# Other places for the modulation chunks, the head sums and the tile splits in the read-out of a two-direction recurrence

## The chip, the cores and the metric

The kernel runs on one core of a Trainium2 chip. The metric is the device time in microseconds (us) of the whole program. The program is cut into stages by barriers at which all engines but SyncE meet, and the change touches three neighbouring stages (the two directions of a recurrence and their read-out).

## The reference, cut to what matters

The reference computes two transformer blocks over 512 tokens of 1024 features. The change lies in the first block. There, modulation vectors (shift, scale and gate of each sublayer) come from the conditioning vector `c`, and a mixer joins an attention half and a gated recurrence that runs in both time directions:

```python
mod_x = (silu(c) @ w_mod[l] + b_mod[l])[:, None, :]
sh1, sc1, gt1, sh2, sc2, gt2 = jnp.split(mod_x, 6, axis=-1)
...
hg_x, hg_c = hgrn2_mixer(px[3:], pc[3:], lb_all[l], hg_norm[l], need_ctx)   # both directions
x = x + gt1 * (concatenate([na_x, hg_x], -1) @ w_out[l])
x = x + gt2 * peer_ffn(modulate(rms_norm(x, norm2[l]), sh2, sc2), ...)

def _gated_out(o, g, norm_g):      # o: sum of both directions, per head
    o = o * rsqrt(mean(o * o, -1) + EPS) * norm_g
    o = o * silu(g)
```

`sh1` and `sc1` are needed at the start of the block. The other four vectors of `mod_x`, which are two thirds of the columns of `w_mod`, are needed only after the recurrence: `gt1` at the output projection, the rest behind it. `peer_ffn` later gathers rows of two tables, `peer_u` and `peer_v`, by index.

## The kernel before

**Weights.** All weights come as one stream of chunks of 512 KB (`in_wstream`), numbered in the order of use. The ring `RING` has four slots (`NSLOT`). SyncE issues the load of chunk c as soon as chunk c-4 has been used, which TensorE reports by the semaphore `chunk_used`. Chunks 48 to 79 are the 32 modulation chunks of the second call (`mod2` and `mod3`), 80 to 87 are the output projection (`out`), and 88 to 103 come after it (`wq`).

**Copies on the same queue.** Behind the load of a chunk SyncE issues copies of the two tables, interleaved row by row, into a DRAM tensor `peer_uv` (L396): each copy takes 1 MB from DRAM to DRAM. From chunk 48 to 79 there is one copy behind each chunk, and two behind each chunk whose number is a multiple of four; from chunk 80 on there is one. These copies are in no hurry, since `peer_uv` is read much later, but they lie in one queue with the loads.

**Modulation** (`modulation`, L611; its matmuls are L617). `modulate(n)` takes the next n of the 32 modulation chunks: 8 matmuls for each chunk with 32 stationary columns (the conditioning) and 128 moving columns from the ring slot, summed up in PSUM bank 6 or 7. It uses no other engine. The author places these calls by hand into gaps of TensorE. Once all 32 are done, ScalarE copies the rows out (`evacuate_rows`, L1146), TensorE turns them (`turn_rows`, L625), and VectorE adds the bias (`add_bias`).

**Two directions** (loop over `d`, one stage each). VectorE runs 24 scans (L1596) and computes 1 - Z (L1598), which sets `ready`. TensorE then makes 16 groups of 8 products (L743), x = 0 to 15; from x = 2 on each waits for VectorE, which scales the operands (L1619, L1620) and takes the last group's result under a mask (`take`, L1608). After each odd x there is one `modulate(1)`. Then TensorE turns six blocks (L756), which ScalarE copies out and VectorE needs to go on, multiplies for the state update (L762), and VectorE carries the state (L1634, L1638) up to the barrier. Before: `modulate(6)` stands ahead of the wait for `ready` in both directions.

**Read-out.** For each of four heads TensorE makes 16 products (L771, L773) into one bank, ScalarE copies and squares it (L1263, L1264). TensorE then runs `modulate(4)` and the four sums over the squares by a matrix of ones (L779). ScalarE takes the four roots (L1115, L1117), VectorE normalises and gates each head (L1647, L1649) and splits the first three chunks of `out` into a high and a low part (`first_chunks`, L1469 and L1471). Barrier 6 follows. Behind it VectorE splits tiles 4 to 7 of `MIX` (the four heads; tiles 0 to 3 were split at the start of the stage; L1485, L1487). TensorE runs eight matmuls that only keep its clock up (`keep_clock`, L634, 512 columns of an identity each), and the tiles of `out` begin (L204 to L206, three passes for each pair of parts).

The order of work on each engine is the order of the program text. Nothing is scheduled by a planner.

Of the kernel before, what the change touches and what calls it, by code (L numbers as in the profile page):

```python
# [20 lines left out]
ALU = mybir.AluOpType  # L21
# [5 lines left out]
KT = D // P  # L27
# [8 lines left out]
HG_HEADS, HG_UNIT = 4, 128  # L36
# [74 lines left out]
def build(nc, t):  # L111
    ctx = ExitStack()
    place = {}
    with ctx:
        def sb(name, shape, dt=F32):
            x = ctx.enter_context(nc.sbuf_tensor(name, shape, dt))
            n = int(np.prod(shape[1:])) * (1 if dt == U8 else 4)
            place[name] = (nc.sbuf_base - n, list(shape))
            return x
# [7 lines left out]
        def sem(name):  # L127
            return ctx.enter_context(nc.semaphore(name))
# [7 lines left out]
        IDN, ONES = sb("IDN", [P, P]), sb("ONES", [P, P])  # L136
# [13 lines left out]
        def bank(b, a=0, n=512):  # L150
            return PS[:, b * 512 + a:b * 512 + a + n]

        def ar(a, n):
            return AR[:, a:a + n]

        def par(name):
            a, n = PCOL[name]
            return PAR[:, a:a + n]
# [12 lines left out]
        def barrier(eng, n):  # L171

            eng.drain().then_inc(phase, 1)  # L173
            eng.wait_ge(phase, 4 * n)
# [41 lines left out]
        G = ar(21504, 2048).rearrange("p (a b) -> p a b", a=4)  # L216
        VW = ar(12288, 4096).rearrange("p (a b) -> p a b", a=4)
        VC = ar(16384, 1024).rearrange("p (a b) -> p a b", a=4)
        MIX = ar(23552, 4096).rearrange("p (a b) -> p a b", a=8)
# [35 lines left out]
        def unit(d, j, h):  # L255

            n = [4, 5, 0, 1, 2, 3][j] if d == 0 else [5, 4, 3, 2, 1, 0][j]
            return (TT * h + n if n < TT else 4 * TT + 2 * h + n - TT), n
# [5 lines left out]
        HLF, HCF, XCF = (x[:].rearrange("p k s -> p (k s)") for x in (HL, HC, XC))  # L264
# [98 lines left out]
        def after(eng, s, key, n, per):  # L363

            eng.wait_ge(s[key], s["use"] * per + n)
# [8 lines left out]
        ho = {k: sem(f"ho_{k}") for k in ("o", "sq", "sum", "root")}  # L374
# [144 lines left out]
        def _(pe):  # L519
# [91 lines left out]
            def modulation(c, which, b):  # L611

                for i in which:
                    weights(pe, c + i)
                for k in range(KT):
                    for i in which:
                        mm = pe.matmul(row_of(bank(b), i), CS[:, 2 * k:2 * k + 32], part(RING, c + i, P * k, P),  # L617
                                       start=(k == 0), stop=(k == KT - 1), skip_group_check=True)
                mm.then_inc(chunk_used, len(which))

            def turn_rows(n, b):

                pe.wait_ge(mod_rows, n + 1)
                for j in range(4):
                    mm = pe.transpose(bank(b, P * j, P), MROWS[n][:, P * j:P * j + P], IDN[:])  # L625
                mm.then_inc(mod_turned, 1)
# [4 lines left out]
            def keep_clock(b, n):  # L631

                for _ in range(n):
                    pe.matmul(bank(b), IDN_R[:], eyes, start=True, stop=True)  # L634
# [91 lines left out]
            def modulate(n):  # L726
                for _ in range(n):
                    i = next(made)
                    modulation(FIRST["mod2"], [i], 6 + i // 16)

            for d in range(2):
                s = hg[d]
                modulate(6)
                after(pe, s, "ready", 1, 1)
                for x in range(16):
                    half = x % 2
                    if x >= 2:
                        after(pe, s, "p", x - 1, 16)
                        after(pe, s, "qk", x - 1, 14)
                    for u in range(8):  # L740
                        a = (8 * half + u) * P
                        lhs, rhs = (Z[d], HQ) if x < 2 else (QK, QK)
                        mm = pe.matmul(PS[:, a:a + P], lhs[:, a:a + P], rhs[:, a:a + P], start=True, stop=True)  # L743
                    mm.then_inc(s["a"], 1)
                    if x % 2 == 1:
                        modulate(1)
                keep_clock(5, 6)
                for n, b in enumerate(HG_BLOCKS):
                    if n == 2:
                        after(pe, s, "p", 16, 16)  # L750
                    if 2 <= n < 5:
                        keep_clock(3, 2)
                    after(pe, s, "kd", n + 1, 6)
                    for j in range(4):
                        a = 512 * b + P * j
                        mm = pe.transpose(PS[:, a:a + P], EW[:, a:a + P], IDN[:])  # L756
                    mm.then_inc(s["kt"], 1)
                after(pe, s, "kz", 6, 6)
                for j in range(5):
                    for h in range(HG_HEADS):  # L760
                        u, n = unit(d, j, h)
                        mm = pe.matmul(bank(j, P * h, P), Z[d][:, u * P:u * P + P], IV[:, n, P * h:P * h + P],  # L762
                                       start=True, stop=True)
                    mm.then_inc(s["u"], 1)
                barrier(pe, 4 + d)

            for h in range(HG_HEADS):
                for n in range(TT):
                    u = (TT * h + n) * P
                    for d in range(2):  # L770
                        pe.matmul(bank(h, P * n, P), IV[:, n, P * h:P * h + P], AT[d][:, u:u + P], start=(d == 0),  # L771
                                  stop=False)
                        mm = pe.matmul(bank(h, P * n, P), SS[d][:, h, n, :], QE[d][:, u:u + P], start=False,  # L773
                                       stop=(d == 1))
                mm.then_inc(ho["o"], 1)
            modulate(4)
            for h in range(HG_HEADS):
                pe.wait_ge(ho["sq"], h + 1)
                pe.matmul(bank((4, 5, 1, 0)[h]), ONES[:], HLF[:, 2048 + 512 * h:2560 + 512 * h], start=True,  # L779
                          stop=True).then_inc(ho["sum"], 1)  # L780
            turn_rows(1, 3)
            turn_rows(2, 4)
            barrier(pe, 6)
            keep_clock(1, 8)

            tiles(FIRST["out"], KT, MIXS, "mix1", main, n2, follow=rms(n2))
            passing(pe, 7)
# [27 lines left out]
            for tt in range(TT):  # L815
                if tt >= 2:
                    pe.wait_ge(po_evac, 2 * (tt - 1))
                for j in range(SLOTS):
                    n = SLOTS * tt + j
                    pe.wait_ge(diag_ready, n + 1)  # L820
                    for x in range(2):
                        mm = pe.matmul(bank(2 * (tt % 2) + x), DIAG[:, n % NDIAG, :],  # L822
                                       ROWS_UV[n % NROW][:, D + 512 * x:D + 512 * x + 512], start=(j == 0),
                                       stop=(j == SLOTS - 1))
# [636 lines left out]
        def _(dve):  # L1461
            steps = Steps(dve, dve_step)
# [12 lines left out]
            def first_chunks(name):  # L1475
                for c in range(ahead):
                    split_chunk(FIRST[name] + c)
# [5 lines left out]
            def split_tile(x, hi, lo, to, n=1):  # L1483

                steps.done(dve.tensor_copy(hi, x))  # L1485
                steps.wait()
                dve.tensor_tensor(lo, x, hi.bitcast(F32), ALU.subtract).then_inc(to, n)  # L1487
# [5 lines left out]
            def split_mix(*which):  # L1493
                for k in which or range(KT):
                    split_tile(MIX[:, k, :], MIXS[0][:, k, :], MIXS[1][:, k, :], x_split)
# [148 lines left out]
            for h in range(HG_HEADS):  # L1644
                o, r = HLF[:, 512 * h:512 * h + 512], EW[:, 512 * h:512 * h + 512]
                dve.wait_ge(ho["root"], h + 1)
                steps.done(dve.tensor_tensor(o, o, r, ALU.mult))  # L1647
                steps.wait()
                dve.scalar_tensor_tensor(MIX[:, 4 + h, :], o, par("hg_norm")[:, h:h + 1], G[:, h, :], ALU.mult, ALU.mult)  # L1649
            first_chunks("out")  # L1650
            barrier(dve, 6)


            split_mix(*range(4, KT))
            for n in (1, 2):
                steps.done(add_bias(n, n + 2))
            steps.wait()
# [156 lines left out]
            for i in range(RET_HEADS * TT):  # L1814
                pair, j = divmod(i // 2, TT)
                h, n = 2 * pair + i % 2, S - P * j
# [108 lines left out]
            for c in range(16):  # L1925
                split_chunk(FIRST["dq"] + c + ahead)
                dve.wait_ge(chunk_used, FIRST["dq"] + c + 1)
                h, by = c % 8, (1.0 if c >= 8 else 0.125)
# [21 lines left out]
            for i in range(n_df + 5):  # L1950
# [16 lines left out]
                if i >= 5:  # L1967
                    k = i - 5
                    o = DO[:, k // TT, P * (k % TT):P * (k % TT) + P]
# [5 lines left out]
                if i % TT == 0 and 1 <= i // TT <= DIFF_HEADS - DLATE:  # L1975
                    h = DLATE + i // TT - 1
# [4 lines left out]
            for h in range(DBY_POOL, DIFF_HEADS):  # L1981
                dve.wait_ge(df["root"], h + 1)
                for ib in range(TT):
                    o = DO[:, h, P * ib:P * ib + P]
# [142 lines left out]
```

## Time and profile before

| | us |
|---|---|
| time before, median of 3 runs | 3511.51 (3508.32 to 3514.45) |
| the profiled execution | 3522.56 |
| its span in the trace | 3520.8 |
| first direction, from barrier 3 to 4 | 390.6 to 480.3 |
| second direction, from barrier 4 to 5 | 480.3 to 563.4 |
| read-out, from barrier 5 to 6 | 563.4 to 599.2 |
| busy in the span: TensorE, VectorE | 3024.0, 2070.3 |

The times in the rows are from the start of the span. The three stages together take 209 us, 6% of the kernel. TensorE has two clocks, and in these stages the granted clock is between 0.64 and 1.00 over stretches of 10 us; a matmul of 512 columns that keeps the clock starts every 0.25 us at the fast one and every 0.45 us at the slow one.

### The profile page before, as it was taken

What the parts mean: (1) busy time and instruction counts of PE and PEld (TensorE: products, weight loads), DVE (VectorE), ACT (ScalarE), POOL (GpSimd) and SP (SyncE); (2) the same over time, 40 slices, a digit from 0 to 9 for tenths busy, and PEclk for the clock granted to TensorE, in tenths of its full rate; (3) what the DMA queues carried; (4) which work ended last, traced back from release to release, by engine and by line L of the source; (5) the groups of instructions that cost most, each with busy time, mean ns of one, the idle gap of its engine ahead of it and who ended that gap; (6) DMA issues with size and microseconds to landing.
All of it is one profiled execution on the core that took longest, in us unless ns stands there. A gap on an engine that the chain in (4) does not pass through costs nothing.

```text
span 3520.8 us, 35290 instructions
## 1 busy us (share of the span) xinstructions
PE 3024.0 (86%) x12520; PEld 2047.1 (58%) x12520; DVE 2070.3 (59%) x3646; ACT 834.3 (24%) x2176; POOL 703.5 (20%) x682
## 2 busy tenths in 40 slices
PE   7999888987777777777777789979999999899998
PEld 5886677762222222222222257667888777778876
DVE  3224785567776764684444455356875465668743
ACT  2112432222222222222222231142120102422201
POOL 0002452014444443343433311000000000100000
PEclk9999999999999999999999999989999999999999
DMA  6999896769999999999999942202333231023332
GB/s 220 317 290 296 242 293 218 234 252 421 421 421 421 408 418 422 413 414 419 419 417 421 415 197 90 78 1 80 99 96 90 78 114 54 12 80 95 95 90 72
DMA packets 154613, 847.89 MB, mean 241 GB/s; under 512 B 15392, under 2 KB 15648, under 8 KB 87648
## 3 DMA queue, kind: packets, MB, share of 16 engines
q0 software_dynamic: 79360, 563.38, 39.3%
q1 hardware_dynamic: 75104, 282.57, 25.9%
q8 instruction: 87, 1.43, 0.2%
q14 instruction: 62, 0.51, 0.0%
HBM read 841.70 MB, written 136.31 MB: 278 GB/s over the span
## 4 chain that ended last, share of the span: by engine, by line
PE 57%; DMA 27%; DVE 8%; issue 4%; ACT 3%; SPq 0%; ACTq 0%; POOL 0%; DVEq 0%; POOLq 0%
DMA RHI_f<-peer_uv,XC 19%; PE PS L204 13%; PE PS L206 13%; PE PS L205 13%; PE PS L822 7%; DMA AR<-peer_uv,XC 5%; DMA RING<-in_wstream 3%; PE PS L597 1%; PE PS L617 1%; DVE AR L1678 1%; DVE RING_r L1471 1%; DVE AR L1608 1%; ACT HC L1315 1%; PE PS L634 1%; DVE AR L1620 1%
## 5 line engine op out<-in xcount | busy, mean ns | idle before, releaser
L822 PE MATMUL PS<-AR,HC 128*128 128x512 f32 x1536 | 726.5, 618 | 256.9 <-ACT HC L1315 256.9
L204 PE MATMUL PS<-AR_r,RHI 128*128 128x512 f32 x1888 | 751.5, 398 | 26.6 <-DVE RING_r L1471 8.9
L206 PE MATMUL PS<-AR_r,RING_r 128*128 128x512 f32 x1888 | 737.7, 391 | 0.0
L822 PEld LDWEIGHTS PS<-AR,HC 128*128 128x128 f32 x1536 | 284.2, 194 | 698.5 <-ACT HC L1315 403.2
L1678 DVE SCALAR_TENSOR_TENSOR AR<-AR 128x1024 f32<-128x1024 f32 x384 | 470.1, 1225 | 366.8 <-DMA AR<-peer_uv,XC 366.2
L205 PE MATMUL PS<-AR_r,RHI 128*128 128x512 f32 x1504 | 586.2, 390 | 0.0
L488 POOL DMA_INDIRECT AR<-peer_uv,XC x384 | 400.3, 1042 | 729.1 <-PE PS L822 547.9
L1469 DVE CAST RHI<-RING 128x1024 fp32r<-128x1024 f32 x256 | 178.4, 697 | 485.4 <-DMA RING<-in_wstream 482.8
L204 PEld LDWEIGHTS PS<-AR_r,RHI 128*128 128x128 f32 x1888 | 356.2, 189 | 111.0 <-issue 21.2
L206 PEld LDWEIGHTS PS<-AR_r,RING_r 128*128 128x128 f32 x1888 | 355.8, 188 | 74.4
L1471 DVE TENSOR_TENSOR RING_r<-RING,RHI 128x1024 fp32r<-128x1024 f32 x256 | 315.8, 1234 | 8.8
L205 PEld LDWEIGHTS PS<-AR_r,RHI 128*128 128x128 f32 x1504 | 282.9, 188 | 62.9 <-issue 6.0
L822 PE MATMUL PS<-RHI_f,HC 128*128 128x512 f32 x512 | 236.7, 605 | 80.8 <-ACT HC L1315 80.8
L1306 ACT ACTIVATE XC<-XC 128x2 f32<-128x2 f32 x256 | 52.1, 203 | 926.6 <-DVE AR L1678 926.6
L1678 DVE SCALAR_TENSOR_TENSOR AR<-RHI_f,AR 128x1024 f32<-128x1024 f32 x128 | 156.6, 1225 | 119.6 <-DMA RHI_f<-peer_uv,XC 119.4
L822 PEld LDWEIGHTS PS<-RHI_f,HC 128*128 128x128 f32 x512 | 92.3, 190 | 225.2 <-ACT HC L1315 133.0
L1315 ACT ACTIVATE HC<-IDN,HC 128x128 f32<-128x128 f32 x512 | 173.7, 386 | 0.0
L488 POOL DMA_INDIRECT RHI_f<-peer_uv,XC x128 | 133.7, 1045 | 186.1 <-PE PS L822 182.3
L205 PE MATMUL PS<-HL_r,RHI 128*128 128x512 f32 x384 | 151.4, 394 | 0.0
L1309 ACT ACTIVATE HC<-XC 128x1 f32<-128x1 f32 x512 | 122.9, 287 | 8.4
L1391 ACT ACTIVATE HL<-PS,PAR 128x512 f32<-128x512 f32 x88 | 67.8, 777 | 228.0 <-PE PS L206 184.4
L506 POOL DMA_DIRECT2D AR<-in_strips x1 | 0.7, 672 | 572.7 <-DVEq L173 572.7
(337 smaller groups left out, 3457.9 us busy)
## 6 DMA issues: line engine op xcount, KB each, us to landing
RING<-in_wstream SPq DMA_DIRECT2D x304, 512.0 KB, 3.6
peer_uv<-in_peer_u SPq DMA_DIRECT2D x56, 1024.0 KB, 14.7
peer_uv<-in_peer_v SPq DMA_DIRECT2D x56, 1024.0 KB, 16.6
peer_uv<-in_peer_v POOLq DMA_DIRECT2D x8, 1024.0 KB, 11.9
peer_uv<-in_peer_u POOLq DMA_DIRECT2D x8, 1024.0 KB, 11.9
AR<-peer_uv,XC POOLq DMA_INDIRECT x384, 13.5
XL<-in_xl SPq DMA_DIRECT2D x1, 2048.0 KB, 8.1
RHI_f<-peer_uv,XC POOLq DMA_INDIRECT x128, 13.5
```

The lines of the kernel that those rows point to most:

```text
L204: pe.matmul(out, sh, mh, start=start, stop=False)
L205: pe.matmul(out, sh, ml, start=False, stop=False)
L206: return pe.matmul(out, sl, mh, start=False, stop=stop)
L488: pool.indirect_dma_start(ROWS_UV[n % NROW], None, PEER_UV, bass.IndirectOffsetOnAxis(ap=IDX[:, n:n + 1], axis=0)).then_inc(row_landed[n % ...
L822: mm = pe.matmul(bank(2 * (tt % 2) + x), DIAG[:, n % NDIAG, :], ROWS_UV[n % NROW][:, D + 512 * x:D + 512 * x + 512], start=(j == 0), stop= ...
L1306: act.activation(GA[:, n:n + 2], RAW[:, n:n + 2], ACT.Gelu).then_inc(gelu, 1)
L1309: act.activation(WEIGHT[:, n + x:n + x + 1], GA[:, n + x:n + x + 1], ACT.Copy, scale=GATE[:, n + x:n + x + 1]).then_inc(weight_ready, 1)
L1315: act.activation(DIAG[:, (n + x) % NDIAG, :], IDN[:], ACT.Copy, scale=WEIGHT[:, n + x:n + x + 1]).then_inc(diag_ready, 1)
L1391: act.activation(HL[:, x, :], bank(x % 4), ACT.Identity, scale=PAR[:, bass.ds(g * BLK + (cw + 2 * 2 * FT + x), 1)], bias=PAR[:, bass.ds(g ...
L1469: dve.tensor_copy(hi, x).then_inc(w_high, 1)
L1471: dve.tensor_tensor(lo, x, hi.bitcast(F32), ALU.subtract).then_inc(w_split, 1)
L1678: dve.scalar_tensor_tensor(JUNK[n % 2], ROWS_UV[n % NROW][:, 0:D], 1.0, HT[:, n // SLOTS, :], ALU.mult, ALU.mult, accum_out=RAW[:, n:n + 1 ...
```

## The change

Five things change, four on TensorE and one on VectorE:

- In direction 0 no modulation chunk comes ahead of `ready`; 36 matmuls of `keep_clock` stand there instead. In direction 1 four chunks stand there, where there were six.
- After the 16 groups, direction 0 takes four more chunks and direction 1 two, both ahead of the transposes; `keep_clock` behind them goes from 6 to 4.
- In the read-out the sum of head h-1 follows the products of head h, and the last sum follows at the end. The remaining modulation chunks, six where there were four, come behind the sums.
- The barrier comes ahead of `turn_rows`, and `keep_clock` behind goes from 8 to 4.
- VectorE splits a head's tile right behind its gating, where it split all four behind the barrier.

The 32 chunks are 14, 14 and 4 before, and 12, 14 and 6 after (direction 0, direction 1, read-out). Nothing changes in SyncE's, ScalarE's or GpSimd's program.

```diff
--- before.py
+++ after.py
@@ -730,7 +730,10 @@
 
             for d in range(2):
                 s = hg[d]
-                modulate(6)
+                if d == 0:
+                    keep_clock(5, 36)
+                else:
+                    modulate(4)
                 after(pe, s, "ready", 1, 1)
                 for x in range(16):
                     half = x % 2
@@ -744,7 +747,8 @@
                     mm.then_inc(s["a"], 1)
                     if x % 2 == 1:
                         modulate(1)
-                keep_clock(5, 6)
+                modulate(4 if d == 0 else 2)
+                keep_clock(5, 4)
                 for n, b in enumerate(HG_BLOCKS):
                     if n == 2:
                         after(pe, s, "p", 16, 16)
@@ -764,6 +768,11 @@
                     mm.then_inc(s["u"], 1)
                 barrier(pe, 4 + d)
 
+            def head_sum(h):
+                pe.wait_ge(ho["sq"], h + 1)
+                pe.matmul(bank((4, 5, 1, 0)[h]), ONES[:], HLF[:, 2048 + 512 * h:2560 + 512 * h], start=True,
+                          stop=True).then_inc(ho["sum"], 1)
+
             for h in range(HG_HEADS):
                 for n in range(TT):
                     u = (TT * h + n) * P
@@ -773,15 +782,14 @@
                         mm = pe.matmul(bank(h, P * n, P), SS[d][:, h, n, :], QE[d][:, u:u + P], start=False,
                                        stop=(d == 1))
                 mm.then_inc(ho["o"], 1)
-            modulate(4)
-            for h in range(HG_HEADS):
-                pe.wait_ge(ho["sq"], h + 1)
-                pe.matmul(bank((4, 5, 1, 0)[h]), ONES[:], HLF[:, 2048 + 512 * h:2560 + 512 * h], start=True,
-                          stop=True).then_inc(ho["sum"], 1)
+                if h >= 1:
+                    head_sum(h - 1)
+            head_sum(HG_HEADS - 1)
+            modulate(6)
+            barrier(pe, 6)
             turn_rows(1, 3)
             turn_rows(2, 4)
-            barrier(pe, 6)
-            keep_clock(1, 8)
+            keep_clock(1, 4)
 
             tiles(FIRST["out"], KT, MIXS, "mix1", main, n2, follow=rms(n2))
             passing(pe, 7)
@@ -1646,12 +1654,13 @@
                 dve.wait_ge(ho["root"], h + 1)
                 steps.done(dve.tensor_tensor(o, o, r, ALU.mult))
                 steps.wait()
-                dve.scalar_tensor_tensor(MIX[:, 4 + h, :], o, par("hg_norm")[:, h:h + 1], G[:, h, :], ALU.mult, ALU.mult)
+                steps.done(dve.scalar_tensor_tensor(MIX[:, 4 + h, :], o, par("hg_norm")[:, h:h + 1], G[:, h, :], ALU.mult,
+                                                    ALU.mult))
+                steps.wait()
+                split_mix(4 + h)
             first_chunks("out")
             barrier(dve, 6)
 
-
-            split_mix(*range(4, KT))
             for n in (1, 2):
                 steps.done(add_bias(n, n + 2))
             steps.wait()
```

On TensorE, from the last work of the attention stage into direction 0 (L709 is that stage's; L743, after L746, are the products; L617 the modulation). Before:

```order
L709 MATMUL PS<-HL,AR 64x128 x8
L617 MATMUL PS<-RING,CS 32x128 x48
L743 MATMUL PS<-AR 128x128 x16
L617 MATMUL PS<-RING,CS 32x128 x8
L743 MATMUL PS<-AR 128x128 x16
```

and after, with the end of the 16 groups of the same direction:

```order
L709 MATMUL PS<-HL,AR 64x128 x8
L634 MATMUL PS<-IDN_R 128x512 x36
L746 MATMUL PS<-AR 128x128 x16
L617 MATMUL PS<-RING,CS 32x128 x8
...
L746 MATMUL PS<-AR 128x128 x16
L617 MATMUL PS<-RING,CS 32x128 x40
L634 MATMUL PS<-IDN_R 128x512 x4
L760 MATMUL PS<-IDN,AR 128x128 x8
```

Six chunks have left the head of the direction, and four of them stand between the last products and the first transposes (x40 is five chunks, where one stood before).

On TensorE, from the last products of the read-out to the first tile of `out`. Before:

```order
L773 MATMUL PS<-AR,HC 128x128
L617 MATMUL PS<-RING,CS 32x128 x32
L779 MATMUL PS<-HL,ONES 128x512 x4
L625 MATMUL PS<-IDN,AR 128x128 x4
L625 MATMUL PS<-IDN,STAT 128x128 x4
L634 MATMUL PS<-IDN_R 128x512 x8
L204 MATMUL PS<-AR_r_57,RHI 128x512
```

and after:

```order
L782 MATMUL PS<-AR,HC 128x128
L773 MATMUL PS<-HL,ONES 128x512 x2
L617 MATMUL PS<-RING,CS 32x128 x48
L625 MATMUL PS<-IDN,AR 128x128 x4
L625 MATMUL PS<-IDN,STAT 128x128 x4
L634 MATMUL PS<-IDN_R 128x512 x4
L204 MATMUL PS<-AR_r_57,RHI 128x512
```

The sums (L779, after L773) now stand ahead of the chunks, two of the four further up among the products, and six chunks stand where four did.

## Rows read from the trace of the kernel before

**Rows 1.** Busy time by stretch, all engines, then granted clock, DMA share and GB/s.

```profile
410.00:475.00 65.00, 58.08 (x439) 52.09 (x438) 53.90 (x51) 21.04 (x26) 37.81 (x30) 0.95 1.02 331
...
568.00:580.00 12.00, 12.00 (x109) 11.88 (x108) 0.00 (x0) 3.69 (x7) 0.00 (x0) 1.00 0.00 1
```

**Rows 2.** Timeline of TensorE, direction 0: start, length, work, [idle before <- releaser].

```profile
390.59 7.66 PE L617 MATMUL PS<-RING,CS 128*32 128x128 f32 x80 [0.44 <-DVEq L173]
407.38 3.62 PE L617 MATMUL PS<-RING,CS 128*32 128x128 f32 x16 [9.13 <-DMA RING<-in_wstream]
410.93 4.87 PE L743 MATMUL PS<-AR 128*128 128x128 f32 x32
464.12 2.01 PE L617 MATMUL PS<-RING,CS 128*32 128x128 f32 x16
466.06 1.65 PE L634 MATMUL PS<-IDN_R 128*128 128x512 f32 x6
467.55 1.03 PE L756 MATMUL PS<-IDN,AR 128*128 128x128 f32 x8
```

**Rows 3.** Timeline of VectorE: the instruction that sets `ready`, in each direction.

```profile
401.06 1.74 DVE L1598 TENSOR_SCALAR AR<-AR 128x3072 f32<-128x3072 f32 x1
...
488.02 1.73 DVE L1598 TENSOR_SCALAR AR<-AR 128x3072 f32<-128x3072 f32 x1
```

**Rows 4.** Timeline of TensorE, direction 1.

```profile
480.32 8.91 PE L617 MATMUL PS<-RING,CS 128*32 128x128 f32 x80 [2.15 <-DVEq L173]
492.62 3.62 PE L617 MATMUL PS<-RING,CS 128*32 128x128 f32 x16 [3.39 <-DMA RING<-in_wstream]
496.17 4.91 PE L743 MATMUL PS<-AR 128*128 128x128 f32 x32
549.16 1.66 PE L634 MATMUL PS<-IDN_R 128*128 128x512 f32 x6
```

**Rows 5.** DMA view, issues at 423.9, 430.5, 466.2, 483.0, 510.0: KB, us to landing.

```profile
RING<-in_wstream SPq DMA_DIRECT2D x1, 512.0 KB, 19.4
RING<-in_wstream SPq DMA_DIRECT2D x1, 512.0 KB, 16.3
RING<-in_wstream SPq DMA_DIRECT2D x1, 512.0 KB, 10.6
RING<-in_wstream SPq DMA_DIRECT2D x1, 512.0 KB, 3.8
RING<-in_wstream SPq DMA_DIRECT2D x1, 512.0 KB, 22.7
```

**Rows 6.** Timeline of TensorE, read-out and first tile of `out`.

```profile
563.40 0.80 PE L771 MATMUL PS<-AR 128*128 128x128 f32 x2 [2.13 <-DVEq L173]
...
579.46 5.95 PE L617 MATMUL PS<-RING,CS 128*32 128x128 f32 x64
585.34 3.70 PE L779 MATMUL PS<-HL,ONES 128*128 128x512 f32 x8
...
599.22 3.78 PE L634 MATMUL PS<-IDN_R 128*128 128x512 f32 x8 [5.97 <-DVEq L173]
602.79 0.63 PE L204 MATMUL PS<-AR_r,RHI 128*128 128x512 f32 x1
```

**Rows 7.** The four chunk loads issued in the read-out: lines of L411, 581 to 586.

```profile
L411 SPq DMA_DIRECT2D RING<-in_wstream x4: 333/334/334, 581.4 to 585.4; - x4
...
DMA to landing us min/median/max: 3.6/10.0/16.2
```

**Rows 8.** Timelines of ScalarE and VectorE in the read-out.

```profile
580.06 0.59 ACT L1264 ACTIVATE HL<-PS 128x512 f32<-128x512 f32 x1
586.50 0.69 ACT L1115 ACTIVATE AR<-PS,PAR 128x512 f32<-128x512 f32 x1 [5.86 <-PE PS L779]
...
592.78 0.75 DVE L1649 SCALAR_TENSOR_TENSOR AR<-HL,PAR,AR 128x512 f32<-128x512 f32 x1
...
599.25 0.43 DVE L1485 CAST AR_r<-AR 128x512 fp32r<-128x512 f32 x1
```

## The prediction, made before the changed kernel had run

> **What bounds the kernel now.** The change lies in three stages, which one barrier after the other keeps in line, so first the timeline of TensorE was read there, then who releases its waits, and then, since a load releases the two longest, the loads themselves. Between the barriers VectorE paces the 16 groups of products. From the first group of direction 0 to its last modulation chunk pass 53.2 us (410.93 to 464.12) [rows 2], and 53.0 us in direction 1 up to the end of its last one (496.17 to 549.16) [rows 4]. The heads of both directions are set by a load. In direction 0 `ready` comes at 402.8 [rows 3], but the sixth chunk lands only at 407.4, and the first products start at 410.93 [rows 2]. In direction 1 `ready` comes at 489.8 [rows 3], the sixth chunk at 492.6, the products at 496.17 [rows 4]. That is 8.1 and 6.4 us which the order of the chunks costs TensorE.
>
> Behind these waits stands a full queue: the DMA engines are at a share of 1.02 from 410 to 475 [rows 1]. On an empty queue a load lands 3.6 to 3.8 us after its issue [rows 5, 7], here after 10.6 to 22.7 [rows 5]. Copies issued between the loads take the time. I number chunks from the program: 59 is the load issued at 423.9, 65 at 466.2, 66 at 483.0, 73 at 510.0, and 80 to 83 are the four of the read-out. Issue plus time to landing gives 443.3 for 59, 476.8 for 65, 486.8 for 66 and 532.7 for 73 [rows 5]. In the read-out the first lands at 585.0 and the fourth at 601.6, so a step of one load and one copy takes 16.6 / 3 = 5.5 us [rows 7]. From 59 to 73 there are 14 steps, four of them with a second copy; they took 33.5 us (59 to 65) and 45.9 us (66 to 73), and the step between, in which the queue ran dry, would have taken some 5.3: 84.7 us, 6.05 a step. The groups use a chunk every 6.5 us (51 to 53 us for eight). The queue and the loop are nearly balanced: what the queue loses by standing idle it cannot make up.
>
> **Direction 0.** Without a chunk ahead, the first group starts with `ready`, at 402.9: **8.0 us earlier**. The 36 clock matmuls hide: at 0.25 us each (six take 466.06 to 467.55 [rows 2]) they end at 399.5. At the slow clock they take 0.45 us (eight take 599.22 to 602.79 [rows 6]), 16.1 in all, and would end at 406.7 and cost 3.8 of the 8.0. I take the fast one, since the chunks that stood there ran at 0.19 us a pair of records, twice as fast as chunk 53's 0.45 [rows 2]. They leave TensorE idle for 3.4 us. Idle gaps of 2.13 and 2.15 us were followed by slow matmuls [rows 4, 6], so I count no gain from the clock in the first groups, which ran at the slow one before as well (4.87 us [rows 2]).
>
> The four added chunks stand between the last products and the transposes, and for these ScalarE waits and then VectorE; no work hides them. Four in a row take 5.9 us (579.46 to 585.34 [rows 6]); two clock matmuls fewer give back 0.5. Transposes, and with them the barrier, come 8.0 - 5.4 = **2.6 us earlier**, and direction 1 starts at 477.7 for 480.3. The last of the four, chunk 59, is issued when 55 has been used, at 458.1, and lands on an empty queue at 461.7; TensorE wants it at 462.4.
>
> **Direction 1.** `ready` comes at 489.75 - 2.6 = 487.1. The queue has been given 60 to 63 by then: four steps of 6.05 behind 461.7 put chunk 63 at 485.9. It is the last of the four ahead of `ready`. TensorE has waited for it for 3 us and takes 3.6 us at the slow clock, like chunk 67 (3.62 [rows 4]). The products start at 489.5, not at 487.1: **6.7 us earlier** than before, not 9.1. 53.0 us later, at 542.5, the loop is done. Two more chunks follow. Chunk 72 is used by 544.0. Chunk 73 is 14 steps behind 59: 461.7 + 84.7 = 546.4. It takes 3.6 us slow, then four clock matmuls 1.8, and the transposes start at 551.8. Before it was 549.16 + 1.49 = 550.65 [rows 2, 4]. So direction 1 gives all of the gain back, and the read-out starts **1.1 us later**, at P = 564.5 (before 563.40 [rows 6]). The reason is in the head of direction 0: the first load went out at 392.5 there, and now goes out when chunk 48 has been used in the loop, at 409.7. The queue stands idle for 17 us more.
>
> **Read-out.** Head sums take 3.70 / 4 = 0.93 us each [rows 6]. Two now lie among the products and put the last square from P + 17.3 (580.65 [rows 8]) to P + 19.1; the last sum follows, and the chunks begin at P + 20.0, before at P + 16.1. The roots begin at P + 19.1 for P + 23.1 (586.50 [rows 8]), 4.0 us earlier. VectorE is done with the heads 7.0 us behind (593.5 [rows 8]), plus four splits of 0.43 + 0.69 [rows 8]: P + 30.6 for P + 30.1. So the earlier sums are paid away by the splits, which before came behind the barrier, where TensorE had 8 us of tiles for which parts were ready.
>
> Then VectorE must split chunks 80, 81 and 82, and barrier 6 waits for that. This is **the largest term**. 82 can be issued only when 78 has been used. Before, 78 and all others had landed, four chunks were used in a row, and 80, 81, 82 were issued from 581.4 and landed by 596.1 [rows 7], 1.2 us ahead of VectorE. Now chunks 78 and 79 are not there: they are issued when 74 and 75 have been used, the first two of the six, and the queue has been dry before, as now [rows 1]. From the start of the chunks to the first issue pass 2.0 us (579.46 to 581.4), then 3.6 to 78, then four steps of 5.5 to 82: P + 20.0 + 2.0 + 3.6 + 22.2 = P + 47.8. One split is 1.9 us (three between 593.5 and 599.2), so the barrier falls at P + 49.7. Before it was P + 35.8 (599.22 [rows 6]): **13.9 us later**. TensorE's and ScalarE's ends, about P + 34, lie under it. `turn_rows` behind the barrier is 1.0 to 1.8 us and four clock matmuls are 1.8, against 3.57 before [rows 6]: 0.3 us less.
>
> **Sum.** 1.1 + 13.9 - 0.3 = 14.7 us later at the first tile of `out`. Behind it the tiles use the first chunk some 16 us later, by when the queue is empty again as before; each stage starts at a barrier, and so the shift goes through to the end. The profiled execution took 3522.56 us, with a span of 3520.8; it lies 11 us over the median, spread over all stages, so I add the difference to the median: 3511.5 + 14.7 = 3526.2 us.
>
> **A rule against the rows.** The read-out's step is 5.5 us by its row [rows 7]. The Trainium skill, "DMA: Bandwidth & Descriptors", section "Anatomy of one DMA — SWDGE (gpsimd) path", fits 2.0 us plus bytes at 436 GB/s to a transfer; a load and a copy of 1.57 MB in all would add 3.6 us a step. The rows don't bear that out as a mean; a copy reads and writes DRAM, and the rate there is what the landings show.
>
> **Rivals.** (A) The queue binds in the read-out alone: loads 63 and 73 are there in time. Then direction 1 starts its products with `ready` at 487.1, the transposes begin at 487.1 + 53.0 + 2.9 + 1.0 = 544.0, and P = 556.8, 6.6 us earlier. The sum is -6.6 + 13.9 - 0.3 = +7.0: 3518.5. For it speaks that 73 misses by only 2.4 us; against it, 63 by 3.
> (B) Not slower: the queue drains faster once copies are thinner spread. The step from the load issued at 423.9 to that at 430.5 was 3.5 us (446.8 - 443.3 [rows 5]). If all were so, no chunk is late in the directions (-6.6), 82 lands at P + 20.0 + 2.0 + 3.6 + 14 = P + 39.6, the barrier is at P + 41.5, and the sum -6.6 + 5.7 - 0.3 = -1.2: 3510.3. This is also what the page's fit would give. Against it stands every mean over more than one step.
> (C) Faster: chunks are never late, barrier 6 waits for VectorE alone, at P + 30.6 + 5.7 = P + 36.3. The sum is -6.6 + 0.5 - 0.3 = -6.4, and 1 or 2 us more if the clock holds: 3504. It needs 82 within 14 us of the first issue, 78 ahead of it.
> (D) More: steps of 5.9 in the read-out (+1.6), 59 issued on a queue that isn't empty, and slow clock in the loops (+6): 3534.
>
> **How the numbers follow.** The forecast has 0.66, A 0.10, B 0.07, C 0.04, D 0.13. The forecast's own range is 3521 to 3531. The range of 8 in 10 takes in A and most of D: 3516 to 3535. A difference of 0.2% (7 us) is about what a measurement of this kernel tells from none. C is the chance of faster, 0.04; B and half of A lie within, 0.12; the rest is slower, 0.84.
>
> **What the profile after would show.** In direction 0 the products start near 402.9, and the first load goes out near 409.7. In direction 1 the fourth chunk (63) waits for its load. Behind the 16 groups of direction 1 the third modulation chunk waits for a load. In the read-out TensorE waits for its last two chunks, and VectorE's splits of 80 to 82 wait for their loads, about 5 us apart; barrier 6 comes about 50 us behind the first product, for 36. The forecast is wrong if VectorE goes from the heads into `first_chunks` without idle time, or if a step of load and copy takes less than 4.5 us.

## The result, and the profile after

| | before | changed |
|---|---|---|
| median | 3511.51 us (3508.32 to 3514.45) | 3527.67 us (3525.45 to 3529.31) |
| ratio | | 1.0044 (95% interval 1.0030 to 1.0059) |
| profiled execution, its span | 3522.56, 3520.8 us | 3529.05, 3527.3 us |

The changed kernel is 16.2 us slower by the medians, where 14.7 us were forecast (3526). Measured again beside the experiments it stood at 1.0043 (1.0026 to 1.0059).

The two traces don't start alike: barrier 3 opens direction 0 at 390.6 us before and at 388.0 after, so times below are taken from there. Each column is one execution. How far single executions differ up to the read-out is shown in the part on why the prediction was right, and it changes how the first rows of this table are to be read.

| us from the start of direction 0 | before | changed | difference | forecast |
|---|---|---|---|---|
| first products of direction 0 | 20.3 | 12.3 | -8.1 | -8.0 |
| VectorE's first masked copy (`take`) | 23.5 | 16.4 | -7.1 | |
| direction 1 starts | 89.7 | 86.1 | -3.7 | -2.6 |
| first products of direction 1 | 105.6 | 101.2 | -4.4 | -6.7 |
| transposes of direction 1 | 160.1 | 158.5 | -1.5 | +1.1 |
| read-out starts (P) | 172.8 | 171.3 | -1.5 | +1.1 |
| barrier 6 | 208.6 | 222.1 | +13.5 | +15.0 |
| first tile of `out` | 212.2 | 225.6 | +13.4 | +14.7 |

TensorE in direction 0 and at the head of direction 1 of the changed kernel (start, length, work, [idle before <- releaser]); these rows answer to [rows 2, 4]:

```profile
387.95 8.46 PE L634 MATMUL PS<-IDN_R 128*128 128x512 f32 x36 [0.44 <-DVEq L173]
400.22 6.46 PE L746 MATMUL PS<-AR 128*128 128x128 f32 x32 [3.81 <-DVE AR L1606]
...
452.71 7.57 PE L617 MATMUL PS<-RING,CS 128*32 128x128 f32 x80
...
461.24 1.03 PE L760 MATMUL PS<-IDN,AR 128*128 128x128 f32 x8
...
474.01 4.90 PE L617 MATMUL PS<-RING,CS 128*32 128x128 f32 x32 [2.14 <-DVEq L173]
479.90 1.93 PE L617 MATMUL PS<-RING,CS 128*32 128x128 f32 x16 [0.99 <-DMA RING<-in_wstream]
485.56 3.62 PE L617 MATMUL PS<-RING,CS 128*32 128x128 f32 x16 [3.72 <-DMA RING<-in_wstream]
```

The wait of 9.13 us for a load at the head of direction 0 is gone; the products wait for L1606, which sets `ready`. In direction 1 two of the four chunks wait for loads, the last for 3.72 us, and it runs at the slow clock as the late ones did before.

The end of direction 1 and the read-out on TensorE, against [rows 4, 6]:

```profile
543.58 1.93 PE L617 MATMUL PS<-RING,CS 128*32 128x128 f32 x16 [0.44 <-DMA RING<-in_wstream]
...
559.23 0.70 PE L780 MATMUL PS<-AR 128*128 128x128 f32 x2 [2.13 <-DVEq L173]
...
578.30 1.12 PE L773 MATMUL PS<-HL,ONES 128*128 128x512 f32 x2 [0.31 <-ACT HL L1272]
579.36 7.57 PE L617 MATMUL PS<-RING,CS 128*32 128x128 f32 x80
591.36 3.62 PE L617 MATMUL PS<-RING,CS 128*32 128x128 f32 x16 [4.43 <-DMA RING<-in_wstream]
610.10 1.11 PE L625 MATMUL PS<-IDN,AR 128*128 128x128 f32 x4 [15.12 <-DVEq L173]
```

VectorE in the same stretch, against [rows 8] (the last head's split, then the splits of chunks 80 to 82):

```profile
589.22 0.69 DVE L1495 TENSOR_TENSOR AR_r<-AR,AR_r 128x512 fp32r<-128x512 f32 x1
596.79 0.69 DVE L1477 CAST RHI<-RING 128x1024 fp32r<-128x1024 f32 x1 [6.88 <-DMA RING<-in_wstream]
...
602.03 0.69 DVE L1477 CAST RHI<-RING 128x1024 fp32r<-128x1024 f32 x1 [3.29 <-DMA RING<-in_wstream]
...
608.04 0.69 DVE L1477 CAST RHI<-RING 128x1024 fp32r<-128x1024 f32 x1 [4.06 <-DMA RING<-in_wstream]
```

And the loads of chunks 78 to 82, issued from 581.3 to 587.0 (the lines of L411 in that window), against [rows 7]:

```profile
L411 SPq DMA_DIRECT2D RING<-in_wstream x5: 333/693/1089, 581.3 to 587.0; - x5
...
DMA to landing us min/median/max: 3.6/12.8/21.1
```

The first lands at 584.9 and the last at 608.1: four steps of 5.8 us, each one load and one copy. VectorE waits 14.2 us in all for the three last of them, and TensorE stands idle for 15.12 us up to barrier 6. Before, VectorE went from the heads into these splits without a pause.

### The profile page after: what moved, and what is told of

Same layout as the page of the kernel before. It is cut to its first block and busy times, and to the rows that moved or that the text cites. A ratio compares the mean times of both kernels' runs of the same rounds, so it can differ in the third digit from the quotient of the medians.

```text
span 3527.3 us, 35347 instructions
## 1 busy us (share of the span) xinstructions
PE 3025.1 (86%) x12548; PEld 2048.1 (58%) x12548; DVE 2071.3 (59%) x3646; ACT 834.5 (24%) x2176; POOL 700.5 (20%) x682
## 5 line engine op out<-in xcount | busy, mean ns | idle before, releaser
L204 PE MATMUL PS<-AR_r,RHI 128*128 128x512 f32 x1888 | 751.2, 398 | 22.7 <-DVE RING_r L1479 7.9
## 6 DMA issues: line engine op xcount, KB each, us to landing
peer_uv<-in_peer_u POOLq DMA_DIRECT2D x8, 1024.0 KB, 16.2
```

Source lines behind the costliest of these rows:

```text
L204: pe.matmul(out, sh, mh, start=start, stop=False)
```

## The experiments

My theory: the queue of the DMA engines sets the ends of these stages, and only where a load stands behind copies and somebody waits for it. The main rival: the new order costs time on the engines themselves. Each run was measured beside the kernel before, and its ratio is to that; it can differ by some 0.0002 from the quotient of two medians, and the interval behind it is of 95%. A microsecond is 0.028 points (per cent).

### The five copies in the way, moved

The changed kernel, with the copies behind chunks 78 to 82 issued behind chunk 91, after which SyncE has nothing to issue for 17 us. Four of the five stand ahead of chunk 82; the fifth comes right behind it.

```diff
         _more = 2 if _c % 4 == 0 and _c < FIRST["out"] else 1
+    if FIRST["out"] - 2 <= _c < FIRST["out"] + 3:
+        _more = 0
+    elif _c == FIRST["wq"] + 3:
+        _more = 6
```

> The changed kernel with one thing else: the five table copies behind chunks 78 to 82 are issued behind chunk 91 instead (six there), where the queue would stand idle. Theory (the read-out waits for loads that stand behind copies): chunks 78 to 82 then land about 1.3 us apart, VectorE doesn't wait for 80 to 82, barrier 6 comes 36.4 us behind the first product of the read-out instead of 50.8, and the kernel takes 3513 us, ratio to the kernel before 1.000. Rival (the new order costs time on the engines themselves, by the splits ahead of the barrier and the chunks behind the sums): no change against the changed kernel, 3527 us, ratio 1.0045.

Measured: 3514.58 us, ratio 1.0004 (0.9995 to 1.0013). TensorE's read-out, the first split of a chunk on VectorE, and the time to landing of the six loads issued from 579.6 to 587.1:

```profile
557.49 0.78 PE L784 MATMUL PS<-AR 128*128 128x128 f32 x2 [2.13 <-DVEq L177]
...
577.62 9.50 PE L621 MATMUL PS<-RING,CS 128*32 128x128 f32 x96
593.87 0.48 PE L629 MATMUL PS<-IDN,AR 128*128 128x128 f32 x1 [6.75 <-DVEq L177]
```

```profile
588.09 0.69 DVE L1481 CAST RHI<-RING 128x1024 fp32r<-128x1024 f32 x1
```

```profile
L415 SPq DMA_DIRECT2D RING<-in_wstream x6: 327/328/334, 579.6 to 587.1; - x6
...
DMA to landing us min/median/max: 3.5/4.4/5.4
```

The engines' instructions and their order are the same; loads land 3.5 to 5.4 us after their issue, all six chunks run through in 9.50 us, VectorE waits for none, and barrier 6 comes 36.4 us behind the first product for 50.9, to the tenth as expected. Taken together the engines' own order costs nothing that can be measured; what makes the changed kernel slower are these copies. Its parts are not each without effect: by the prediction the early sums gain 4.0 us and the splits ahead of the barrier cost 4.5, and a run further down, with four chunks at the end and without those splits, has barrier 6 at 30.5 us. The run doesn't tell either whether the loads were late because they stood behind the copies in SyncE's order or because both shared the DMA engines at that time; no run moved the copies to another queue.

The same move in the kernel before:

> The kernel before with the five copies behind chunks 78 to 82 issued behind chunk 91, and nothing else. It tells whether moving these copies is a gain by itself. Theory (a copy costs only where somebody waits for the load behind it): in the kernel before chunk 82 landed 1.2 us ahead of VectorE, so nothing is gained, barrier 6 stays 35.8 us behind the first product, ratio 1.000. Rival (less traffic there helps in general, and gave the 14 us in the changed kernel): faster by 5 us or more, ratio 0.998 or less.

Measured: 3513.66 us, ratio 0.9997 (0.9986 to 1.0007). Barrier 6 stays where it was, 35.9 us behind the first product (560.06 to 595.94). So it isn't that less traffic there helps in general. The copies cost 14 us only in an order in which somebody waits behind them.

### One part of the change alone: the early head sums

The kernel before, with the sums among the products and `modulate(4)` behind them:

```diff
                 mm.then_inc(ho["o"], 1)
-            modulate(4)
-            for h in range(HG_HEADS):
-                pe.wait_ge(ho["sq"], h + 1)
...
+                if h >= 1:
+                    head_sum(h - 1)
+            head_sum(HG_HEADS - 1)
+            modulate(4)
```

> The kernel before with one part of the change alone: each head's sum follows the next head's products, and the four chunks come behind the sums. Theory (loads set the barrier): the roots start 4.0 us earlier, but the loads of chunks 80 to 82 are issued 3.9 us later, chunk 82 lands 36.7 us behind the first product and barrier 6 comes at 38.6 for 35.8: 2.8 us slower, ratio 1.0008. Rival (the chain of sums, roots and VectorE sets it): 4.0 us faster, ratio 0.9989.

Measured: 3518.77 us, ratio 1.0016 (1.0006 to 1.0025). TensorE, then VectorE's splits of 81 and 82:

```profile
555.35 0.49 PE L776 MATMUL PS<-AR 128*128 128x128 f32 x2 [2.13 <-DVEq L173]
...
593.14 3.78 PE L634 MATMUL PS<-IDN_R 128*128 128x512 f32 x8 [11.98 <-DVEq L173]
```

```profile
586.05 0.69 DVE L1473 CAST RHI<-RING 128x1024 fp32r<-128x1024 f32 x1 [4.52 <-DMA RING<-in_wstream]
...
591.09 0.69 DVE L1473 CAST RHI<-RING 128x1024 fp32r<-128x1024 f32 x1 [3.09 <-DMA RING<-in_wstream]
```

Barrier 6 is 37.8 us behind the first product for 35.8. These 2.0 us lie at the lower end of what the ratio says (2 to 9 us). A step that makes the roots start 4 us earlier makes the kernel slower, since it puts off the chunks that release the loads. Then with both edits, sums and moved copies:

> The kernel before with the early head sums (as in the run that had this part alone, 1.0016) and the five copies moved. Theory: without copies ahead of chunks 80 to 82 the earlier roots are worth their 4.0 us, barrier 6 comes 31.9 us behind the first product for 35.8, and the ratio is 0.999, 0.27 points under the run without the move. Rival (the early sums cost by their own work): 1.0016 again.

Measured: 3509.68 us, ratio 0.9982 (0.9973 to 0.9991). The first product is at 554.40 and TensorE goes on behind barrier 6 at 584.87:

```profile
584.87 3.78 PE L638 MATMUL PS<-IDN_R 128*128 128x512 f32 x8 [4.66 <-DVEq L177]
```

Barrier 6 comes after 30.5 us, 1.4 less than expected: the products began at the fast clock here (0.49 us for the first row, as against 0.80 in [rows 6]). The early sums are a gain, and in the changed kernel the copies and the splits hid it.

### The splits behind the barrier again

```diff
-                steps.done(dve.scalar_tensor_tensor(MIX[:, 4 + h, :], o, par("hg_norm")[:, h:h + 1], G[:, h, :], ALU.mult,
-                                                    ALU.mult))
-                steps.wait()
-                split_mix(4 + h)
+                dve.scalar_tensor_tensor(MIX[:, 4 + h, :], o, par("hg_norm")[:, h:h + 1], G[:, h, :], ALU.mult, ALU.mult)
             first_chunks("out")
             barrier(dve, 6)
+            split_mix(*range(4, KT))
```

> The changed kernel with the splits of the four head tiles back behind barrier 6. They take 4.5 us of VectorE ahead of the barrier. Theory (loads set the barrier): nothing is gained, VectorE waits 4.5 us longer for chunk 80 instead, ratio to the kernel before 1.0045. Rival (the engines' own work sets it): 4.5 us faster than the changed kernel, ratio 1.003.

Measured: 3535.0 us, ratio 1.0064 (1.0052 to 1.0077). Nothing was gained, and VectorE shows why: its wait for chunk 80 has grown by what the splits had taken.

```profile
584.23 0.75 DVE L1657 SCALAR_TENSOR_TENSOR AR<-HL,PAR,AR 128x512 f32<-128x512 f32 x1
596.01 0.69 DVE L1477 CAST RHI<-RING 128x1024 fp32r<-128x1024 f32 x1 [11.03 <-DMA RING<-in_wstream]
```

But 1.0064 is more than the theory had, and so the kernel was run once more, now beside the changed one, whose expectation stands second:

> The changed kernel with the splits of the four head tiles behind barrier 6 once more, now beside the changed kernel. It was measured at 1.0064 where the theory wants the changed kernel's ratio. Theory (nothing is gained or lost, loads set the barrier): within 0.1% of the changed kernel. Rival (the splits behind the barrier delay the first tile or its successors): some 7 us above it again.

> The changed kernel itself, beside the others, as a yardstick on this chip. Every theory: ratio 1.0044 as measured, within 1.003 to 1.0059.

Measured: 3531.55 us, ratio 1.0051 (1.0034 to 1.0068), and the changed kernel 3528.87 us, 1.0043 (1.0026 to 1.0059). The difference of 0.08 points is within the intervals. The rival's gain of 4.5 us is excluded; a small loss is not, and the first measurement's excess stays unexplained. Its profile shows none: barrier 6 is 48.3 us behind the first product, as in the second trace of the changed kernel (48.3), but the profiled execution was the fastest of the five (3528.3 us). In the repeat it is at 50.3.

### The chunks of direction 0 ahead of `ready`

```diff
-                if d == 0:
-                    keep_clock(5, 36)
-                else:
-                    modulate(4)
+                modulate(4)
+                if d == 0:
+                    keep_clock(5, 12)
...
-                modulate(4 if d == 0 else 2)
+                if d == 1:
+                    modulate(2)
```

> The changed kernel with the four chunks of direction 0 taken ahead of ready (they have landed) and followed by 12 clock matmuls, instead of behind the 16 groups. Theory (idle time of the queue at the head comes back as waits): the first loads go out 17 us earlier, direction 1 never waits for a load, its products start 9.4 us behind barrier 4 instead of 15.1, and with the 5.4 us of the tail saved the kernel is some 11.5 us faster than the changed one: 3516 us, ratio 1.0013. Rival (only the place in the tail costs): 5.4 us faster, 3522 us, ratio 1.003. The read-out stays at 50.8 us in both.

Measured: 3518.07 us, ratio 1.0011 (1.0002 to 1.0020).

```profile
387.88 5.96 PE L617 MATMUL PS<-RING,CS 128*32 128x128 f32 x64 [0.44 <-DVEq L173]
...
468.28 5.95 PE L617 MATMUL PS<-RING,CS 128*32 128x128 f32 x64 [2.14 <-DVEq L173]
477.77 5.46 PE L745 MATMUL PS<-AR 128*128 128x128 f32 x32 [3.53 <-DVE AR L1606]
```

The four chunks of direction 1, which took 15.1 us with their waits in the changed kernel, take 5.95 us, and products start 9.5 us behind barrier 4, with `ready`. The first loads went out at 389.8 and not at 408.6. The first tile of `out` comes 215.0 us after the start of direction 0, for 225.6 in the changed kernel: 10.7 us, where 11.5 were expected and the rival had 5.4. Of these, 2.6 lie in the read-out, which the edit doesn't touch (barrier 6 at 48.3 for 50.9); against the second trace of the changed kernel, whose read-out takes 48.3 too, the gain is 9.7 us, all of it ahead of the read-out. So the idle stretch of the queue at the head of direction 0 came back as waits in direction 1.

### A version from the theory

Both directions take four chunks ahead of `ready`, none ahead of the transposes, and one behind the state products; the sums stay early, the splits go behind the barrier, the five copies behind chunk 91:

```diff
-                modulate(4 if d == 0 else 2)
                 keep_clock(5, 4)
...
                 mm.then_inc(s["u"], 1)
+                modulate(1)
                 barrier(pe, 4 + d)
```

> A version made by the theory. Both directions take four chunks ahead of ready (direction 0 with 20 clock matmuls behind them), eight in the groups, none ahead of the transposes and one behind the state products, where TensorE waits 2.1 us for barrier 4 or 5. The read-out keeps the early sums and the six chunks at its end, the splits of the head tiles are behind barrier 6, and the five table copies behind chunks 78 to 82 are issued behind chunk 91. Theory: products start with ready in both directions (14.4 us earlier in all), nothing is added to the tails, barrier 6 comes 31.9 us behind the first product for 35.8: 18.6 us faster than the kernel before, less 1 for slow clock, 3496 us, ratio 0.995. Rival (loads are late whatever the order, since the queue carries the same work): the gains come back as waits in direction 1, ratio 0.999 or more.

> The same version with all table copies where they are in the kernel before. Theory: P is 14.4 us earlier, but chunk 82 stands behind four copies again, barrier 6 comes some 49 us behind the first product for 35.8, and the kernel is about where the kernel before is, ratio 1.000; the difference to the version with moved copies is 17 us. Rival (copies don't hold up loads; the order alone matters): the same time as with moved copies, 0.995.

Measured: with moved copies 3500.57 us, ratio **0.9964** (0.9949 to 0.9978), with all copies in their places 3515.98 us, 1.0004 (0.9994 to 1.0015). Five copies are worth 0.40 points here, 14 us. Barrier 6 comes 33.4 us behind the first product with them moved (546.38 to 579.75) and 48.4 with them in place (545.49 to 593.91). The version beats both kernels, by the interval 8 to 18 us against the one before, where 17.6 were expected. The 33.4 are 1.5 more than expected, since VectorE still waited 3.2 us for chunks 80 and 81. Its chunk behind the state products costs nothing: TensorE is released by barrier 4 after 0.28 us idle for 2.15 [rows 4].

```profile
468.71 5.95 PE L621 MATMUL PS<-RING,CS 128*32 128x128 f32 x64 [0.28 <-DVEq L177]
478.20 6.48 PE L749 MATMUL PS<-AR 128*128 128x128 f32 x32 [3.54 <-DVE AR L1609]
```

### The clock ahead of the products

In that version the first products of direction 1 took 6.48 us after 3.54 us idle. In direction 0, where 20 clock matmuls left 1.54 us, they took 3.84. One edit, `keep_clock(5, 20 if d == 0 else 12)`:

> The version with covered chunks and moved copies (0.9964), with 12 clock matmuls behind the four chunks of direction 1. They take 3.0 of the 3.5 us for which TensorE stands idle ahead of its products. In that version the first two groups took 6.48 us after 3.5 us idle in direction 1 and 3.84 us after 1.5 us idle in direction 0. Theory (the idle gap costs the clock): the two groups take 3.84 us in direction 1 too, 2.6 us faster, ratio 0.9957. Rival (the slow groups lie under VectorE's work): no change, 0.9964.

Measured: 3503.18 us, ratio 0.9961 (0.9946 to 0.9977); no change. The clock was held, and it was worth nothing:

```profile
480.96 3.84 PE L748 MATMUL PS<-AR 128*128 128x128 f32 x32 [0.59 <-DVE AR L1608]
```

From these products to the first of the read-out pass 68.2 us (480.96 to 549.17), and 68.2 without the edit (478.20 to 546.38). My theory fell here, and the rival was right. VectorE shows it, in the version without the edit:

```profile
480.18 2.29 DVE L1611 TENSOR_TENSOR AR<-AR 128x2048 f32<-128x2048 f32 x1 [2.04 <-ACT AR L1251]
482.39 1.30 DVE L1619 COPY_PREDICATED AR<-HL,PS 128x1024 f32<-128x1024 uint8 x1
```

The first masked copy follows VectorE's own multiply without a pause. Where products start with `ready`, VectorE is the later of the two whatever TensorE's clock is.

## Why the prediction was right, point by point

**What bounds.** Right: the queue of loads and copies, at the head of direction 1 and in the read-out. The profile showed every wait that was named: chunk 63 in direction 1, chunk 73 behind its groups (0.44 us only), chunk 79 and the splits of 80 to 82 in the read-out. Chunk 62, not named, was waited for too (0.99 us).

**How far one pair of traces carries.** Three runs of the kernel before leave everything up to the read-out as it is (moved copies, early sums, both), and so do four of the changed one (moved copies, the splits behind the barrier twice, the kernel itself again). Their traces give the first three rows; the last row has those alone whose read-out is that of its kernel, or for the kernel before the one with moved copies:

| us | before: its trace; others | changed: its trace; others | forecast of the difference |
|---|---|---|---|
| direction 0 | 89.7; 86.5 to 86.6 | 86.1; 86.2 to 86.8 | -2.6 |
| direction 1 | 83.1; 82.3 to 83.6 | 85.2; 84.3 to 86.5 | +3.7 |
| start of direction 0 to P | 172.8; 168.9 to 170.0 | 171.3; 171.1 to 172.9 | +1.1 |
| P to barrier 6 | 35.8; 35.9 | 50.9; 48.3 | +13.9 |

The first work of TensorE in direction 0, direction 1 and the read-out, in the kernel before with moved copies and then in the changed kernel again, there with the work behind barrier 6:

```profile
390.02 7.61 PE L621 MATMUL PS<-RING,CS 128*32 128x128 f32 x80 [0.44 <-DVEq L177]
476.50 7.66 PE L621 MATMUL PS<-RING,CS 128*32 128x128 f32 x80 [2.14 <-DVEq L177]
560.06 0.49 PE L775 MATMUL PS<-AR 128*128 128x128 f32 x2 [2.13 <-DVEq L177]
```

```profile
389.10 8.46 PE L634 MATMUL PS<-IDN_R 128*128 128x512 f32 x36 [0.44 <-DVEq L173]
475.54 3.27 PE L617 MATMUL PS<-RING,CS 128*32 128x128 f32 x32 [2.15 <-DVEq L173]
562.00 0.49 PE L780 MATMUL PS<-AR 128*128 128x128 f32 x2 [2.13 <-DVEq L173]
610.26 1.12 PE L625 MATMUL PS<-IDN,AR 128*128 128x128 f32 x4 [14.50 <-DVEq L173]
```

The trace of the kernel before is the slow one up to P, by 2.8 to 3.9 us against the three others, most of it in direction 0. So the -3.7 and -1.5 us of the result's table are for the most part not the change: against the three others direction 0 gave nothing, direction 1 lost some 2.4 us, and P came 2.3 us later. The forecast of +1.1 was near for a reason that it didn't have: direction 0 gave 2.6 us less than forecast, and direction 1 cost 1.3 us less.

**Direction 0.** In the pair of traces the head was right to a tenth for TensorE (-8.1), but the term was taken at the wrong engine. VectorE's first copy moved by 7.1 only, since it now comes behind VectorE's multiply (L1608 in the changed kernel), while before it waited for the late products. The slow clock of the first groups (6.46 us), which the sum left out, lies under that multiply and costs nothing, as the last run showed for direction 1. The tail was sized at 5.4 us and came to 3.5 (from VectorE's first copy to the transposes 53.4 before, 56.9 after): the last group of products ran at the fast clock after 1.27 us idle, where in the trace before it ran at the slow one (3.53 us after 1.87). Together -3.7 for -2.6. In the three other traces of the order before, VectorE's first copy comes at 22.7 us and the transposes 51.1 us behind it; in the five of the changed order at 16.4, and 56.9 to 57.7 behind. So the head is worth 6.3 us there and the tail costs 5.8 to 6.6, and the 2.6 us of gain are not there. The term was off because it was read at TensorE, while VectorE sets the pace.

**Direction 1.** Chunk 59 was forecast to land 71.1 us after the start of direction 0 and landed at 70.3, 63 at 95.3 and landed at 97.6, 73 at 155.8 and landed at 155.6. Counting steps in the queue thus held within 2.3 us over 85 us. The late 63 put off the products by 2.3 us against the forecast (101.2 for 98.9), and with them the time at which TensorE wanted 73. As 73 landed when it should, its wait shrank from 2.4 us to 0.44, and TensorE stayed at its fast clock. The term that was mis-sized is the 3.6 + 1.8 us at the slow clock behind 73: the chunk and the four matmuls behind it took 2.9 us (543.58 to 546.48), 2.5 less, and that is why the transposes came 2.6 us ahead of the forecast in spite of the later start. The four other traces bear this out: chunk 63 was used 97.8 to 98.2 us after the start of direction 0, while 73 was waited for in two of them only, for 1.0 and 1.7 us, and the four clock matmuls behind it ran at the fast clock each time (1.2 us).

**Read-out.** The largest term was right. The chunks begin 20.1 us behind the first product (20.0 forecast), the first issue is at 22.1 (22.0), chunk 82 lands at 48.9 (47.8), barrier 6 is at 50.9 (49.7). The step of load and copy was 5.8 us for 5.5, which is nearly all of the 1.2 us. In the five other traces with six chunks and the copies in place, four steps took 22.1 to 22.7 us, 5.5 to 5.7 each, and barrier 6 came 48.3 to 50.3 us behind the first product. Behind the barrier the forecast had 0.3 us less, and it was 0.1.

**Sum.** +13.4 us in the traces for +14.7; the medians say 16.2, with an interval from 10.5 to 20.7. The rest of the two traces differs by 7 us the other way, of which 2.6 lie ahead of the changed stages: single executions of this kernel differ by that much in stages that are the same in both. Between the changed kernel's second trace and the kernel before with moved copies, barrier 6 moves by 15.2 us (221.2 for 205.9). The 13.9 us of the read-out were found by their mechanism. That the sum came within 1.5 us of the medians is in part luck, since the errors in the two directions cancelled.

**Rivals.** A (only the read-out binds) would have had +7.0; the wait of 3.72 us for chunk 63 says no, though in its other half, chunk 73 in time, it was nearly right. B and C needed steps of 3.5 us or none; four steps took 23.2 us. D (more) had nearly its steps of 5.9 us in this one trace, but not its slow loops or a late chunk 59.

By an estimate from the fit in the Trainium skill, "DMA: Bandwidth & Descriptors", section "Anatomy of one DMA — SWDGE (gpsimd) path", a step would have taken 3.6 us; the traces have 5.5 to 5.8, so here the measurement decides. The section is about transfers that GpSimd issues, and these are issued by SyncE. Whether that or the copies' way from DRAM to DRAM makes the difference, no run here shows.

## What to carry to other kernels

Work that releases a load can cost more than its own duration: before it is put later, ask which load it releases, what else stands in that queue, and who waits for the last load of the row. Bulk transfers without a deadline belong behind the loads of a stretch in which nobody waits, not among those of the one that ends a stage; here five of them, of which four stood ahead of the last load, were worth 14 us. And a step that is taken out of the critical path (the head sums, 4 us) can only be judged once what comes last behind it has been looked at.

## What the runs showed of the hardware

- In the read-outs a load of 512 KB behind one copy of 1 MB from DRAM to DRAM landed 4.2 to 6.7 us behind the load ahead of it, in the mean of four steps 5.5 to 5.8 us. Without copies loads landed 3.5 to 5.9 us after their issue, even where six were issued within 7.5 to 8.0 us.
- TensorE's clock was slow behind some short idle stretches, and not behind each of the same length: after 1.87 us in direction 0 of the kernel before the next group ran at the slow clock (3.53 us), while in the version with covered chunks a group after 1.87 us idle ran at the fast one (2.02 us). Over all traces it was slow in three and fast in four. After 3.3 to 3.8 us the groups that followed were slow each time (5.28 to 6.48 us for two), after 1.5 us never (3.84).
- Where another engine comes later anyway, the slow clock costs nothing: 6.48 or 3.84 us for the same two groups gave the same 68.2 us up to the read-out.
